# A triangular inverse on 32 columns per head, and the first output projection as three rounded passes

## What is computed

```python
hm = hm.transpose(0, 2, 1, 3).reshape(B, S, W) * head_norm_g
y_m = jax.nn.sigmoid(o) * hm
y_p = multiscale_pool(u, pool_w, pool_scale)
return jnp.concatenate([y_m, y_p], axis=-1) @ w_out      # (256, 1024) @ (1024, 1024)
```

```python
A = jnp.where(tri_strict, jnp.einsum('bhncd,bhnmd->bhncm', kb, kc) * decay, 0.0)
lhs = A + jnp.eye(C)
sol = lax.linalg.triangular_solve(lhs, rhs, left_side=True, lower=True, unit_diagonal=True)
```

## Time and profile before

| | us |
|---|---|
| median of 3 runs | 1648.52 (1648.29 to 1649.6) |
| the profiled execution | 1648.02 |
| its span (first to last instruction) | 1646.3 |
| mean granted TensorE clock, share of full speed | 0.998 |
| TensorE busy | 1624.4 (99% of the span) |
| VectorE busy | 613.7 (37%) |
| ScalarE busy | 475.8 (29%) |
| GpSimd busy | 302.4 (18%) |

### The profile page before, as it was taken

How to read it: one execution, slowest core, us unless ns; L and a number is a source line. 1 busy time by engine, 2 the same in 40 slices (tenths; PEclk the granted TensorE clock), 3 DMA queues, 4 the chain that set the end, 5 groups by cost and what they waited for, 6 DMA issues and landing times. The chain is left out here.

```text
span 1646.3 us, 22758 instructions
## 1 busy us (share of the span) xinstructions
PE 1624.4 (99%) x9272; PEld 946.4 (57%) x9272; DVE 613.7 (37%) x1144; ACT 475.8 (29%) x695; POOL 302.4 (18%) x192
## 2 busy tenths in 40 slices
PE   9999999999999999999999999999999999999998
PEld 8843333333333333333333333698998999999986
DVE  7743212112121212121121211675485244468852
ACT  5421110111111111111011111574555454454443
POOL 3500000000000000000000000535333624445552
PEclk9999999999999999999999999999999999999999
DMA  9698999999999999999999999353133215456552
GB/s 350 221 367 338 428 427 426 428 427 426 428 426 427 429 426 427 426 428 428 428 428 428 428 428 422 125 179 128 53 123 134 103 52 195 166 166 203 167 192 102
DMA packets 92919, 507.67 MB, mean 308 GB/s; under 512 B 8987, under 2 KB 32584, under 8 KB 68264
## 3 DMA queue, kind: packets, MB, share of 16 engines
q1 hardware_dynamic: 92696, 506.00, 76.1%
q10 hardware_dynamic: 144, 0.52, 0.1%
HBM read 505.46 MB, written 1.05 MB: 308 GB/s over the span
## 5 line engine op out<-in xcount | busy, mean ns | idle before, releaser
L186 POOL TENSOR_TENSOR low<-ring,high 128x1024 fp32r<-128x1024 f32 x81 | 199.6, 2465 | 1262.8 <-ACT high L183 1262.7
L1593 PE MATMUL ps<-ring,x 128*64 128x512 f32 x1536 | 337.5, 594 | 1.8 <-DMA ring<-in_w_up 1.8
L1593 PEld LDWEIGHTS ps<-ring,x 128*64 128x64 f32 x1536 | 108.0, 137 | 227.5 <-issue 222.4
L183 ACT CAST high<-ring 128x1024 fp32r<-128x1024 f32 x162 | 168.2, 1047 | 201.4 <-PE ps L1727 125.5
L1720 PE MATMUL ps<-hTh,high 128*128 128x256 f32 x800 | 198.8, 285 | 2.4 <-DVE hTl L633 1.9
L1721 PE MATMUL ps<-hTl,high 128*128 128x256 f32 x800 | 197.6, 284 | 0.0
L1626 PE MATMUL ps<-ring,x 128*64 128x512 f32 x752 | 171.7, 598 | 0.0
L186 DVE TENSOR_TENSOR low<-ring,high 128x1024 fp32r<-128x1024 f32 x81 | 111.1, 1371 | 146.7 <-ACT high L183 146.6
L1720 PEld LDWEIGHTS ps<-hTh,high 128*128 128x128 f32 x800 | 153.9, 192 | 4.2 <-issue 3.8
L1721 PEld LDWEIGHTS ps<-hTl,high 128*128 128x128 f32 x800 | 154.0, 192 | 0.0
L1466 DVE TENSOR_SCALAR hT<-ps 128x512 f32<-128x512 f32 x32 | 22.1, 692 | 295.8 <-PE ps L1593 295.8
(11 more groups left out here) (465 smaller groups left out, 2181.7 us busy)
## 6 DMA issues: line engine op xcount, KB each, us to landing
ring<-in_w_down SPq DMA_DIRECT2D x52, 2048.0 KB, 20.5
ring<-in_w_gate SPq DMA_DIRECT2D x48, 2048.0 KB, 18.2
ring<-in_w_up SPq DMA_DIRECT2D x48, 2048.0 KB, 18.5
ring<-in_w_in SPq DMA_DIRECT2D x23, 2048.0 KB, 8.2
extra<-in_w_gate SPq DMA_DIRECT2D x16, 2048.0 KB, 18.9
extra<-in_w_up SPq DMA_DIRECT2D x16, 2048.0 KB, 17.5
extra<-in_w_down SPq DMA_DIRECT2D x14, 2048.0 KB, 21.0
ring<-in_w_up SPq DMA_DIRECT2D x22, 1024.0 KB, 7.4
```

The costliest lines, as they stand in the source:

```text
L183: eng.copy(hi, self.raw(u)).then_inc(self.sem("high_split"), 1)
L186: eng.tensor_tensor(lo, self.raw(u), hi.bitcast(F32), ALU.subtract).then_inc(self.sem(who + "_split"), 1)
L1593: last = pe.matmul(bank[h * CAP:(h + 1) * CAP, :], xg[:, c, kh, :], w[:, c, h * 512:(h + 1) * 512], start=False, stop=kh == 1 and c == 3)
```

## The change

It has two parts, independent of each other.

**The projection.** `w_out` is now split in eight pairs of chunks: `out_pair(n, q)` names the buffers of half `n` and chunks 2q and 2q + 1. Some are the three split buffers, others parts of `hTh_first` and `hTl_first` and of the new `yTl_first`, which are free by then. ScalarE makes the eight high parts, VectorE three low parts (`OUT_LOW0`), GpSimd five. The activation is split too: ScalarE's scaled copy is the high part, a VectorE operation gives the low one. TensorE does three passes for each pair and each half of the tokens. SyncE's list changes: pieces 4 and 5 go when the pairs are split instead of when TensorE has finished, and the three late pieces change places, so that the bias tables, which go ahead of the last late piece, now come last.

**The inverse.** Up to blocks of 32 (levels 1 to 4), `X` is kept compact: the inverse is block diagonal, so each matrix has only 32 columns per row that can differ from zero (`Xc`). One mask (`near`) serves all these levels, and VectorE applies the level's mask to the compact product (`below_c`). The transposed `XT` is no longer made by TensorE: VectorE transposes four bands of 32 by 32 blocks. Level 5 (`FINE`) and level 6 compute only the blocks that are not zero, with 32 and 64 columns.

The core of the diff, in the order of the file:

```diff
+    OUT_LOW0 = ((0, 3), (1, 2), (1, 1))
...
+    def out_high(act, n, q):
+        ring.landed(act, OUT0 + n)
+        splits.made("high", ("out", n, q), act.copy(out_pair(n, q)[0], out_raw(n, q)))
+
+    def out_low(eng, n, q):
+        who = "low0" if (n, q) in Splits.OUT_LOW0 else "low1"
+        hi, lo = out_pair(n, q)
+        splits.wait(eng, "high", ("out", n, q))
+        splits.made(who, ("out", n, q), eng.tensor_tensor(lo, out_raw(n, q), hi.bitcast(F32), ALU.subtract))
...
-            for n, use in ((0, ("qk", 3)), (1, ("v", 1)), (2, ("u", 1)), (3, ("o", 1)), (Pieces.LATE[2], ("o", 1)), (Pieces.LATE[1], ("pool", 1)),
-                           (6, ("ym", 1)), (7, ("ym", 1)), (4, ("out", 0, 1)), (5, ("out", 1, 1)), (Pieces.LATE[0], ("out", 1, 1))):
-                banks.done(sp, use)
+            for n, use in ((0, ("qk", 3)), (1, ("v", 1)), (2, ("u", 1)), (3, ("o", 1)), (Pieces.LATE[0], ("pool", 1)),
+                           (6, ("ym", 1)), (7, ("ym", 1)), (4, None), (5, None), (Pieces.LATE[1], ("out", 1, 1)),
+                           (Pieces.LATE[2], ("out", 1, 1))):
+                if use is not None:
+                    banks.done(sp, use)
+                else:
+                    sp.wait_ge(sem("low0_split"), LOW0_UNITS + (1 if n == 4 else 3))
+                    sp.wait_ge(sem("low1_split"), LOW1_UNITS + (4 if n == 4 else 5))
...
+            out_high(act, 0, 2)
+            out_high(act, 1, 3)
+            for j in range(2):
+                y_high(2 + j, ("pool", j), P1["pool_scale"] + 2 * j)
...
+            out_pair_used(act, 0)
+            out_high(act, 0, 0)
+            out_pair_used(act, 1)
+            out_high(act, 0, 1)
+            for j in range(2):
+                y_high(j, ("ym", j), P1["head_norm_g"] + 2 * j)
+            out_high(act, 1, 0)
+            out_high(act, 1, 1)
...
+            for n, q in ((0, 2), (1, 3), (0, 0), (0, 1), (1, 0)):
+                out_low(g, n, q)
...
-            pooled_half(0, 0)
-            pooled_half(0, 1)
-            pooled_half(1, 0)
+            pooled_half(0, (3, 2))
+            pooled_half(1, (2, 3))
...
-                for l in range(1, LEVELS):
+                for l, to, w in ((FINE, Tc, R), (FINE + 1, Tw, 2 * R)):
                     for t in range(NT):
...
+                        if l == FINE:
+                            banks.moved(act, ("xx", hg, l - 1, t))
+                            act.copy(Xw[:, t, :, 0:R], Xc[:, t])
+                            act.activation(Xw[:, t, :, R:], Xc[:, t], ACT.Copy, scale=odd_row[:, 0:1])
                         bank = banks.take(act, ("t1", hg, l, t))
...
+                for l in range(1, FINE):
+                    for t in range(NT):
+                        bank = banks.take(v, ("t1", hg, l, t))
+                        last = v.scalar_tensor_tensor(Tc[:, t], fine(bank), -1.0,
+                                                      below_c[:, l - 1, :].unsqueeze(1).to_broadcast([P, HG, R]),
+                                                      ALU.mult, ALU.mult)
+                        banks.release(last, ("t1", hg, l, t))
+                    for t in range(NT):
+                        bank = banks.take(v, ("xx", hg, l, t))
+                        banks.release(v.tensor_tensor(Xc[:, t], Xc[:, t], fine(bank), ALU.add), ("xx", hg, l, t))
+                        banks.moved(v, ("xx", hg, l, t))
+                        for rows in blocks():
+                            last = v.transpose(XT[rows, t, :, rows], Xc[rows, t])
+                        last.then_inc(sem("x1T"), 1)
...
+                            for h in range(HG):
+                                last = pe.matmul(bank[:, h * R:(h + 1) * R], XT[:, t, h, :], Tc[:, t, h, :],
+                                                 start=True, stop=True)
```

More of the change, by code:

```diff
@@ L684, in phase_a @@
     inv = part(1, 8 * S, 4, S)
-    uT = yT[:, 0:4, :]
+    uT = part(0, 0, 4, S, of=spare)
     DT = part(0, 8 * S, NT, NH, S)
@@ L816, in _, with y_high @@
                 banks.release(last, ("o", t))
[L818 to L824, removed]
+            def y_high(j, key, scale):
+                bank = banks.take(act, key)
+                for i in range(2):
+                    last = act.activation(yTh[:, 2 * j + i, :], bank[:, i * S:(i + 1) * S], ACT.Copy,
+                                          scale=prm1[:, scale + i:scale + i + 1])
+                splits.made("high", ("y", j), last)
+            out_high(act, 0, 2)
+            out_high(act, 1, 3)
+            for j in range(2):
+                y_high(2 + j, ("pool", j), P1["pool_scale"] + 2 * j)
             k.prepare(act)
@@ L992, in _, with y_low @@
             splits.ahead(v, "low0", 20)
+            out_low(v, 0, 3)
+            out_low(v, 1, 2)
+            def y_low(j, key, scale):
+                bank = banks.take(v, key)
+                splits.wait(v, "high", ("y", j))
+                for i in range(2):
+                    c = 2 * j + i
+                    last = v.scalar_tensor_tensor(yTl[:, c, :], bank[:, i * S:(i + 1) * S], prm1[:, scale + i:scale + i + 1],
+                                                  yTh[:, c, :].bitcast(F32), ALU.mult, ALU.subtract)
+                    if i == 0:
+                        chain.mark(last)
+                    else:
+                        banks.release(last, key)
             for j in range(NT):
@@ new lines, in _ @@
+                for t in range(NT):
+                    bank = banks.take(v, ("xx", hg, FINE, t))
+                    for rows in blocks(True):
+                        last = v.tensor_copy(Xw[rows, t, :, 0:R], fine(bank)[rows])
+                    banks.release(last, ("xx", hg, FINE, t))
+                    bank = banks.take(v, ("xt", hg, FINE, t))
+                    for b in (0, 2 * R):
+                        last = v.tensor_copy(XT[b:b + R, t, :, b + R:b + 2 * R], fine(bank)[b:b + R])
+                    banks.release(last, ("xt", hg, FINE, t))
@@ L2254, in _ @@
+                for t in range(NT):
+                    bank = banks.take(v, ("xt", hg, FINE + 1, t))
+                    wide = bank[0:2 * R, 0:HG * 2 * R].rearrange("p (h n) -> p h n", h=HG)
+                    banks.release(v.tensor_copy(XT[0:2 * R, t, :, 2 * R:], wide), ("xt", hg, FINE + 1, t))
                 for h in range(HG):
```

225 lines of the change are left out of this document (142 added, 83 removed).

## The result

The changed kernel takes 1683.53 us (median of 4 runs, 1682.42 to 1685.18), the kernel before 1648.4 in the same session: a ratio of 1.0214 with a 95% interval of 1.0198 to 1.0229, or 35 us more. The sign and the mechanism that the prediction put first were right; the time lies 10 us above the range. The profiled execution took 1685.18 us with a span of 1683.5.

What follows compares the result with a forecast made beforehand. TensorE was taken to bound the kernel, busy 99% of the span. Forecast: -2.2 us for the projection plus 2 x 10 for the inverses, 1648.5 + 17.8 = 1666.3 us; own range 1657 to 1674, with both large cases 1635 to 1673.

Steps and rivals of the forecast that it cites:

- The sign and the mechanism that the prediction put first: Both inverses: narrow records let TensorE's clock fall to 1.2 GHz, so the kernel gets slower, 1666.3 us; chance 0.50.
- The step on which it rested: Inverse levels: each record has its own load of 128 columns, 0.11 us, so 32 moving columns aren't 4 times cheaper.
- if it lasts 3 us into the logits, 12.5: Behind each inverse: the low clock lasting 3 us into the attention logits makes a group cost 12.5 us more.
- the main sum: Whole kernel: -2.2 us for the projection plus 2 x 10 for the inverses, +17.8, giving 1666.3 us.
- the two waits behind the transposes: Output projection: TensorE waits 1.1 us for ScalarE's first scaling and 1.1 us for GpSimd's low part of (1, 0).
- the four splits ACT makes before the scalings fit its idle time: Ahead of the output projection: ScalarE's four early weight splits fit its idle time; first pass at 85.4, 0.8 us later.
- I take nothing for it: Loads before the first expert: five of 2 MB from 97 end by 122, the sixth by 128; no time counted.
- The rival: First expert: bias tables, queued behind LATE[1], arriving after its bias matmuls would lose a few us; no chance given.
- The clock stays: Both inverses: clock kept at 2.4 GHz, VectorE bounding the levels, 1637 to 1640.3 us, say 1638.7; chance 0.36.
- The cheap end: Inverse at full clock: 0.2 us a transpose, 3.7 us a level, four levels 16 us, a group 23.7 us.
- A dear transpose: Inverse, clock kept: each 0.1 us more per VectorE transpose costs 6.4 us; at 0.54, 1656 us; chance 0.10.
- Cheap loads: Inverse: the clock falls but weight loads don't slow; 5 us or so of the gain lost, 1643 us; chance 0.04.

Runs made afterwards that it cites:

- the inverse alone: The kernel before with only the inverse half of the change, all edits from `near, far` on: 1676.58 us, ratio 1.0171.
- The run with a wide level 6: Against the inverse alone, only the first product of level 6 reads its columns twice over (128 columns): 1666.38 us, ratio 1.0105 to the kernel before.
- The run that makes it come true for the inverse: Against the inverse alone, levels 1 to 5 read their 32 columns four times, level 6 its 64 twice: 1643.68 us, ratio 0.9974 to the kernel before.

## Why the prediction was right and wrong

**Right: the inverse.** It was forecast at 38.4 us a group by a fall of the clock after one level, 6.8 us a level and doubled loads; it took 37.8 (1154.19 to 1191.95), with 6.83 a level and 0.21 us a load. The step on which it rested, that 128-column loads and not the moving side set a record's pitch, holds at both clock levels. That the fall would come at all was in part luck. It was taken from one fall behind products of few rows, and whether few rows do it is still open; here few columns did. The two runs at 128 and at 32 columns, equal in records and loads, are what shows the cause.

The Trainium skill ("TensorE: Matmul & The Clock Gate", section "Why this matters for your kernels") names gaps of idle time as what brings the lower clock. The trace agrees in the first mixer, where the clock fell 1.2 us behind a gap of 3.22 us and stayed up when ones filled it, and at the first expert, where it fell in the wait of 1.66 us, behind one of 1.37. The rule doesn't cover the inverse. There the clock fell and stayed down with TensorE busy all the time (in the inverse alone), and it stayed up, at 128 columns, with waits of 0.24 and 0.43 us in every level.

**Wrong in size: what follows a fall.** The step "if it lasts 3 us into the logits, 12.5" was the upper end of the range. It lasted 11 us into them (in the profile of the inverse alone 6 in one group and 11 in the other), and a group cost 9.4 + 5.2 = 14.6 us (with the transposes ahead taken off) instead of 10. That is 9 us of the 17 by which the forecast missed. The working had no row for how long the clock stays low; its 3 us were a bound without a reason, and the main sum took nothing at all for it. The run with a wide level 6 puts the price at 10.2 us for both groups.

**Wrong in sign: the projection.** Forecast at -2.2 us with bounds of -5.4 and +0.8, it is +6.3. Its passes cost what was said at the full clock (0.23 each), and so did the two waits behind the transposes, nearly (1.1 and 1.1 us forecast, 0.99 and 0.56 measured). The terms that failed:
- The step that costed ScalarE's and VectorE's early splits at nothing ("the four splits ACT makes before the scalings fit its idle time"). VectorE's did fit VectorE's idle time, but slowed GpSimd, whose chain TensorE waits for: 1.8 us, and the clock's fall behind the longer gap. Taking it away gives 2.2 us back; filling the gap 3.1.
- The step "I take nothing for it" on the loads. The rival was named with its place, the tables behind the first expert's bias matmuls, and then priced at nothing because the loads would be done by 128. They started late: the first of them left at 103.6 and not at 97, since it waits for the transposes, which TensorE reached at 102.5 and not at 96.5, and pieces 4 and 5 left at 106.3 and not from 100. The exchange of two entries gives back 4.4 us.
- No step let the clock fall at a wait. It did at two of them, at the low level from about 87 to 93 us and from 135 to 141.

That the queue had nothing to do before the late start is seen in one row, a window of the kernel after (the last two numbers are the DMA share and GB/s):

```profile
96.00:104.00 8.00, 7.63 (x38) 6.11 (x36) 0.00 (x0) 2.36 (x3) 2.58 (x2) 1.00 0.00 0
```

**The rivals.** "The clock stays" was priced at 1638.7, with VectorE as the bound at 3.7 to 4.2 us a level. The run that makes it come true for the inverse gives 4.75 a level: a transpose takes 0.31 (four in 1.25 us), not 0.27, which is 0.34 us for eight, and the working had one of VectorE's two products in the chain (0.27 for the 0.49 that both take). The cheap end was also added up wrong: four levels at 3.7 are 14.8 us, not 16. The inverse was worth 4.5 us, against 6 to 9.4. Here the Trainium skill ("VectorE: DVE Perf Modes", section "Two Vector instructions with no wait between them") was the better guide: one instruction that starts in another quadrant waits for all before it, and the four transposes, in four quadrants, start 0.31 us apart, each after the other's full 0.30, while the two products, which start in the same quadrant, take 0.29 each and start 0.20 apart. "A dear transpose" had its mechanism right and its size wrong. "Cheap loads" is refuted by 0.21 us a load.

## What to carry to other kernels

Columns that are cut from a matmul save nothing where each has its own load of 128 columns: here a record took 0.11 us at 32, 64 and 128 columns. Worse, the narrow matmuls can cost the clock, here 6.8 us a level instead of 4.75 and 5 us more behind each inverse, and reading the same columns four times over gave it back at no cost in time. When a forecast has a fall of the clock in it, look for the next piece of work that would end the fall, and price the stretch up to there. Work moved into an engine's idle time still shares something with its neighbours: look at what a third engine does in those microseconds, and who waits for it.

## What the runs showed of the hardware that I hadn't expected

- A GpSimd copy of 6 columns takes a full 1 us longer beside a VectorE subtraction of 1024 columns, though it moves next to nothing. The profile of before has such a row too, beside VectorE's splits of 69 to 74 us; it was there to be read before an early split was costed at nothing:

```profile
69.92 1.19 POOL L890 COPY extra<-spare 128x4 f32<-128x4 f32 x1
```

- The clock fell on records of 32 columns with TensorE busy throughout (at about 1151 in the inverse alone) and stayed low over 16.00 busy us of 16.00; it fell at 64 columns too, and held at 128 with the same records and loads.
- A fall costs far beyond its cause: behind the inverse 11 us at the low level, behind the 1.66 us wait for the tables 3.1 us more in the expert's first products.
- A short fall at products of 4 or 8 rows comes in some executions and not in others: at 42 us it is in the profiled execution of the changed kernel, not in that of the kernel before. It moves a profile's later rows by 1 to 2 us, so two profiles are best compared by the distances between their places.
